# 232 products that nobody reads, put where TensorE waits in the routing and at the head of two attention stages

## The reference, cut to what matters

```
for i in range(DEPTH):                       # DEPTH = 2
    h = rmsnorm(x, g_mix[i])
    u = h @ w_in[i]
    y_a = stick_breaking_attention(...)      # 8 heads of 64
    y_b = differential_attention(...)        # 4 heads
    x = x + merged @ w_o[i]
    # mixture of experts, 4 groups of 8, top 2, hidden 256
    g_sel = argmax(t @ w_rg + b_rg)
    top_p, top_i = top_k(softmax(e_logits[rows, g_sel]), 2)
    expert_id = g_sel * 8 + top_i
    ...                                      # tokens sorted into blocks of their expert
    x = x + segment_sum(gate * expert(x))
    x = x + (p[i] @ w_ple[i]) * ple_gate
# then, once: the second kind of layer
h = rms_norm(x, g_mix); z = h @ w_in         # window attention, recurrence, block attention, merge, ffn
```

## Time and profile before

| | us |
|---|---|
| median of 3 runs | 2697.54 (2697.39 to 2698.08) |
| the profiled execution: its time | 2694.89 |
| the profiled execution: its span | 2693.1 |
| TensorE busy | 2366.4 (88% of the span) |
| VectorE busy | 996.3 (37%) |
| ScalarE busy | 570.0 (21%) |
| GpSimd busy | 405.4 (15%) |
| mean granted clock of TensorE | 0.940 |

### The profile page before, as it was taken

How to read it: one execution, slowest core, us unless ns; L and a number is a source line. 1 busy time by engine, 2 the same in 40 slices (tenths; PEclk the granted TensorE clock), 3 DMA queues, 4 the chain that set the end, 5 groups by cost and what they waited for, 6 DMA issues and landing times. The chain is left out here.

```text
span 2693.1 us, 29813 instructions
## 1 busy us (share of the span) xinstructions
PE 2366.4 (88%) x11776; PEld 1741.3 (65%) x11776; DVE 996.3 (37%) x1728; ACT 570.0 (21%) x1165; POOL 405.4 (15%) x402
## 2 busy tenths in 40 slices
PE   4888789958988898879987988869999999999998
PEld 3666578834445666648864444668776888788886
DVE  3344423431113444442352111445564333422234
ACT  2342310211112233230030111222344000200011
POOL 1101011112211110101111221111110111112111
PEclk9999889979998899969998999889999999999999
DMA  5302033579993211103277997343221333233221
GB/s 164 104 24 65 24 83 94 220 294 412 414 404 139 85 50 40 49 16 104 82 285 313 415 414 321 126 114 88 78 81 42 100 96 112 80 98 97 94 94 70
DMA packets 291553, 402.98 MB, mean 150 GB/s; under 512 B 31306, under 2 KB 230730, under 8 KB 273478
## 3 DMA queue, kind: packets, MB, share of 16 engines
q1 hardware_dynamic: 276444, 373.31, 39.0%
q0 software_dynamic: 10176, 16.81, 1.7%
q10 hardware_dynamic: 4778, 10.76, 1.5%
HBM read 388.99 MB, written 30.15 MB: 156 GB/s over the span
## 5 line engine op out<-in xcount | busy, mean ns | idle before, releaser
L130 PE MATMUL banks<-h_split,w_high 128*128 128x512 f32 x2624 | 832.3, 398 | 7.9 <-DVE w_low L182 5.1
L130 PEld LDWEIGHTS banks<-h_split,w_high 128*128 128x128 f32 x2624 | 489.6, 190 | 116.3 <-DVE w_low L182 5.5
L182 DVE TENSOR_TENSOR w_low<-w_raw,w_high 128x1024 fp32r<-128x1024 f32 (+1 forms) x264 | 316.6, 1199 | 582.9 <-POOL w_high L171 582.8
L130 PE MATMUL banks<-h_split,w_low 128*128 128x512 f32 x1312 | 518.2, 395 | 0.0
L171 POOL CAST w_high<-w_raw 128x1024 fp32r<-128x1024 f32 (+1 forms) x264 | 274.6, 1040 | 1616.8 <-PE banks L130 1424.2
L130 PEld LDWEIGHTS banks<-h_split,w_low 128*128 128x128 f32 x1312 | 249.0, 190 | 55.7
L130 PE MATMUL banks<-w_high,op_split 128*128 128x512 f32 x736 | 231.2, 394 | 0.4 <-DVE mg_part L1046 0.3
L1569 PE MATMUL banks<-expert_ring,ex_xsT 128*64 128x256 f32 x1472 | 179.0, 398 | 18.4 <-DMA expert_ring<-in_w_exp_up 15.5
L130 PEld LDWEIGHTS banks<-w_high,op_split 128*128 128x128 f32 x736 | 138.2, 188 | 33.4 <-issue 0.9
L1569 PEld LDWEIGHTS banks<-expert_ring,ex_xsT 128*64 128x64 f32 x1472 | 106.8, 143 | 76.6 <-DMA expert_ring<-in_w_exp_up 17.2
L130 PE MATMUL banks<-w_low,op_split 128*128 128x512 f32 x368 | 144.8, 393 | 0.0
(11 more groups left out here) (391 smaller groups left out, 2767.0 us busy)
## 6 DMA issues: line engine op xcount, KB each, us to landing
w_raw<-in_w_in SPq DMA_DIRECT2D x142, 512.0 KB, 4.0
expert_ring<-in_w_exp_gate SPq DMA_DIRECT2D x46, 1024.0 KB
expert_ring<-in_w_exp_up SPq DMA_DIRECT2D x46, 1024.0 KB
expert_ring<-in_w_exp_down SPq DMA_DIRECT2D x46, 1024.0 KB
w_raw<-in_w_gu SPq DMA_DIRECT2D x44, 512.0 KB, 4.0
region<-in_w_exp_gate SPq DMA_DIRECT2D x20, 1024.0 KB
region<-in_w_exp_up SPq DMA_DIRECT2D x20, 1024.0 KB
region<-in_w_exp_down SPq DMA_DIRECT2D x20, 1024.0 KB
```

Source lines behind the costliest of these rows:

```text
L130: last = nc.tensor.matmul(out, left, right, start=(start and n == 0), stop=(stop and n == 2), skip_group_check=True)
L182: self.nc.vector.tensor_tensor(self.low[:, i % self.SPLIT, 0:n], self.raw[:, i % self.RAW, 0:n], self.high[:, i % self.SPLIT, 0:n].bitcast ...
```

## The change

A helper issues `n` products of 128 x 128 by 128 columns, all of the same two constants, into one bank that nobody reads at that point. It waits for nothing and signals nothing. It is called with 28 at the head of `stick_breaking` and of `window_attention`, and with 36, 48 and 64 in the routing: after the embedding's transposes, after the ranks, and after the table. `stick_breaking` and the routing run twice, so there are 2 x (28 + 36 + 48 + 64) + 28 = 380 such products in a run, from 204 in the code of TensorE.

```
+def keep_busy(k, bank, n):
+
+    for _ in range(n):
+        k.nc.tensor.matmul(k.ps[:, bank, 0:P], k.ident_r[:], k.neg_tri[:], start=True, stop=True)
...
                 last.then_inc(pv_done, 1)
 
+            keep_busy(k, 7, 28)
             norm.open(pe)
...
             last.then_inc(p_turned, 1)
-
+            keep_busy(k, 1, 36)
 
             pe.wait_ge(member_ready, 1)
...
             last.then_inc(ranked, 1)
-
+            keep_busy(k, 1, 48)
             pe.wait_ge(block_hot_ready, 1)
...
             last.then_inc(tabled, 1)
+            keep_busy(k, 1, 64)
...
                 last.then_inc(pv_step, 1)
 
+            keep_busy(k, 5, 28)
             norm.open(pe)
```

## The result

The changed kernel takes 2708.76 us against 2697.47 us of the kernel before (medians of six runs each), 11.3 us slower. The ratio estimated from all the runs is 1.0047, with a 95% interval of 1.0035 to 1.0059; it lies a little above the ratio of the two medians (1.0042), and one of the six runs took 2720.88 us. The forecast was 12.0 us slower. The trace holds 380 unread products, from 204 in the code; the title's 232 is neither of these numbers.

A forecast was written before the change was run, and what follows sets the result against it. VectorE's chain and TensorE's small jobs bound the routing, memory the experts' stage. Losses of 10.8 (routings) + 0 + 0.8 + 0.4 (heads) = 12.0 us bring 2697.5 to 2709.5 us; range 2699 to 2716.

The forecast's parts named there:

- The pace: TensorE, each unread product: 0.11 us at clock 1.00 and 0.214 us at 0.50, the latter from L1279's products.
- The ranks: Routing, five products after the 36: still run at the higher clock and end 0.5 us earlier.
- The fall of the clock: Routing: the clock outlasts the 36, falls to 0.50 near 549 and stays down while unread products run.
- the first break: Routing, TensorE's wait of 1.3 us between the 36 and `member`, behind which the clock was to fall.
- I take them to be the weaker kind: TensorE: unread products, taking 256 columns' time with only 128 passing, raise the clock less than equally dense transposes.
- The 48 and the table: Routing: the 48 at 0.50 take about 10.1 us, end at 558.7; the table ends at 560.6, 2.4 us late.
- The drain follows the table: Routing's end: GpSimd's fetches and drain shift with the table, the drain to 570.9, 2.4 us late.
- The faster rival: Clock holds in the routing and rises at the heads: -2.6 to -11.2 us, about -7, 2690.5 us; chance 0.14.
- The 64 and the entry: Routing's end: the 64 take 13.7 us, TensorE is last at the barrier, experts' transposes start 5.7 us late.
- `gate_up`: First experts' products: mostly at 0.50 as before, 0.3 us taken off for some work at 1.00, leaving 5.4 a layer.
- The experts' stage: After the routing: runs at the memory's pace, so a shift of the first `gate_up` shifts the whole stage.
- The heads: Three heads, 28 products at 0.50 taking 6.0 us: losses of 0, 0.8 and 0.4 us.

The follow-up runs named there:

- the last group alone: The changed kernel with only the 64 unread products behind the routing's table, the other groups removed; ratio 1.0027 to the kernel before.
- the routing alone: The changed kernel with only the 36, 48 and 64 unread products, none at the heads; ratio 1.0048 to the kernel before.
- the 28 alone: The changed kernel with only the 28 unread products at each head, the 36, 48 and 64 removed; ratio 0.9999 to the kernel before.
- the kernel with 27 and 6: The changed kernel with 512-column products: 14 at each head, 27 behind the table, 6 ahead of the first `gate_up`; ratio 0.9973 to the kernel before.

## Why the prediction was right, point by point

- **The pace.** 0.117 us at 1.00 (4.22 for 36) and 0.217 at 0.50 (13.88 for 64), where I took 0.11 and 0.214. L1279 was the right row. (Its (1.92 - 0.41) / 7 is 0.216 and not 0.214; 0.1 us on the 64.) The Trainium skill (TensorE: Matmul & The Clock Gate, LDWEIGHTS) would have 107 ns at the lower clock; the trace has twice that, and by the page's figure the loss would have been missed.
- **The ranks.** 0.73 us in place of 1.25, the 0.5 saved as forecast; the wait ahead of them 1.13 for a forecast 1.3.
- **The fall of the clock.** Forecast near 549, found near 550.5; less the 1.1 us by which this routing began later, that is 549.4. The reason given, the first break, is at most half of it: with transposes in place of the products the clock held over breaks of 1.19 and 1.73 us. The step that carried the forecast was the other one, "I take them to be the weaker kind", and the runs with transposes and with 512 columns bear it out. Its ground does not hold, though: "the time of 256 columns with only 128 passing" is true of the transposes as well, at the same 0.117 us apiece, and they keep the clock. So the step was right by some luck, and what makes these products the weaker kind stays open. The Trainium skill (same page, Why this matters for your kernels) asks for a TensorE that is kept busy without long pauses; here, from 550.6 to 573.6, it was busy without a pause and stayed at 0.50.
- **The 48 and the table.** They end 1.8 and 2.0 us later against the embedding's transposes than before (forecast 2.4), since the first 0.8 us of the 48 (549.72 to 550.5) ran fast.
- **"The drain follows the table."** This step is wrong, and it did not show, because TensorE was later still. In every kernel where TensorE is not last, the entry follows SyncE's last load more closely (12.3 to 13.9 us behind it) than the end of the table (10.9 to 13.7), and that load waits for the store of the normalized rows; why the fetches end with the load is inferred, not shown. The faster rival had -0.8 a layer from it, which the table at 1.00 did not bring in any kernel.
- **The 64 and the entry.** TensorE last at the barrier, 0.89 to the transposes (taken 0.8), which are 5.3 and 5.4 late (forecast 5.7).
- **`gate_up`.** I took 0.3 off. It went the other way: 6.38 and 6.24 us in place of 5.39 and 5.63, since the clock came back 5.5 us behind its start (584.7 against 579.14). Before it came back within 3.3 to 4.3 us: the stretch from 576 to 577 has a mean of 0.87, the one from 577.5 on 1.00. This is the term that was mis-sized: 6.25 and 5.97 a layer in place of 5.4, 12.2 for the 10.8. The unread products are not needed for it. With the last group alone, behind the same 64, `gate_up` takes 5.50 and 5.51 us; with longer code and no unread product in the routing it takes 5.14 in the first layer and 6.24 in the second, where the store is longer and the entry later (27.6 us behind the store's issue in place of 26.4) and the clock comes back 5.0 in place of 3.0 us behind its start. So its length moves with the moment of the entry, both ways, and a price for a shift has to allow a microsecond a layer for it.
- **The experts' stage** did not pass the shift on in full in the first layer (7.4 in, 5.6 out) and did in the second (11.2 in, 11.8 out). In the other kernels the shift moves by up to 3.5 us within this stage, both ways (with the routing alone 6.8 in and 10.3 out; in the 512-column kernel 1.3 in and -0.2 out), so no more than this can be read from one execution.
- **The heads.** 0.9 and 0.6 us later at the first product, forecast 1.65 and 0.6, taken 0.8 and 0.4. At the second head the clock rises 0.8 us behind the first product (919.2), where it took 2.2 (911.89 to 914.1), so most of the 0.9 is returned. The sum of the second head was also 0.2 too high: free at 904.0, 28 x 0.214 ends at 910.0, not 910.2. By the start of the work behind each head's first products the net loss is 0.2 and 0.4 us, 0.6 in place of the 1.2; with the 28 alone no change was measured, to within 5 us.

The mechanism was right where the money is: the clock fell, neither the 48 nor the 64 fitted, TensorE was last at the barrier, and the routing lost 12.2 us for the 10.8 forecast. That the sum came within a microsecond (12.8 us by the two spans, 11.3 by the medians) is partly luck: the routings cost 1.4 us more than forecast, the heads 0.6 less, and shifts that no term of the prediction covers, each between -1.8 us (the first experts' stage) and +1.1 (ahead of the first routing), cancelled one another.

## What to carry to other kernels

A filler has to be tried for what it does to the clock, not for how busy it keeps TensorE: 64 narrow fp32r products kept it busy for 13.9 us at 0.50, while products with 512 columns held 1.00 over the whole routing. Size each group to its wait at the clock that it will have, and count as gain only what follows the wait that ends last, here `gate_up` and not the small jobs in between. And before pricing a small job, look for the transfer that the barrier really waits for: a longer drain with an earlier start gives it away.

## What the runs showed of the hardware

- At one pace (0.117 us apiece at 1.00), fp32 transposes of 128 x 128 held the clock at 1.00 over waits of 1.19 and 1.73 us, and fp32r products of 128 x 128 by 128 columns did not hold it over 1.13, while with 512 columns (0.24 us apiece) they held it over 1.35; at 0.50 these did not raise it in 13.8 us without a pause, and wide fp32r products did within 5.0 us: the 27 of the kernel with 27 and 6 began at 0.50 (559.49) and ran at 1.00 from 564.5. Which property of the product counts is not shown.

```profile
559.60:564.00 4.40, 4.40 (x12) 3.44 (x12) 2.80 (x13) 0.00 (x0) 2.03 (x2) 0.50 0.98 357
564.50:568.00 3.50, 3.50 (x16) 2.63 (x14) 0.00 (x0) 0.00 (x0) 0.00 (x0) 1.00 0.99 401
```

- Code can have a cost apart from its time on the engine. Instructions come in packets of 16 KB (queue q8: 100 packets with 1.64 MB before, 103 with 1.69 MB with the change, which lengthens the code of TensorE alone) through the DMA engines that also move the data. Where one such packet fell 7.5 to 13 us behind the issue of the 2 MB store, the store was 1.2 to 1.5 us longer in nine of ten cases, 14.4 to 14.8 in place of 13.1 to 13.6 us, and SyncE's next load as much later. The tenth case, and one code-only case alone among the nine, leave the cause likely but not proven. The Trainium skill (Runtime: NRT & Kernel Launch, Instruction fetch mechanics) tells of 16 KiB blocks that each engine fetches itself, at a cost that is mostly hidden. The size agrees with the packets here; hidden it was not, where others waited for the store.
